# Score products of a streaming encoder's attention on 32 or 64 rows, two maps as a pair

## What is computed

```python
# B, per query block: keys selected by the indexer's top k
s = jnp.einsum('bqhd,bqkhd->bqhk', q, k_sel).astype(jnp.float32) * (B_HEAD_DIM ** -0.5)
p = jax.nn.softmax(jnp.where(valid[:, :, None, :], s, -jnp.inf), axis=-1)
...
# C, per query block: two maps i = 0, 1 of 32 channels per head
s = jnp.einsum('bqhid,bkhid->bhiqk', q, k).astype(jnp.float32) * (C_HALF ** -0.5)
p = jax.nn.softmax(jnp.where(mask, s, -jnp.inf), axis=-1)
attn = (p[:, :, 0] - lam * p[:, :, 1]).astype(v.dtype)
o = jnp.einsum('bhqk,bkhe->bqhe', attn, v)
```

## Time and profile before

| | us |
|---|---|
| median of 3 runs | 2077.38 |
| range of the runs | 2076.96 to 2079.85 |
| span of the profiled execution | 2076.9 |
| busy: TensorE | 1871.0 |
| busy: VectorE | 1235.4 |
| busy: ScalarE | 538.1 |
| busy: GpSimd | 311.5 |

### The profile page before, as it was taken

One profiled execution on the slowest core, in us unless ns is written; L12 is line 12 of the kernel. 1 busy time (PEld: TensorE's weight loads), 2 busy tenths in 40 slices (PEclk: granted clock), 3 DMA queues, 4 the chain that ended last, 5 costly groups with the idle time before them and its releaser, 6 DMA issues. The chain is left out here.

```text
span 2076.9 us, 21666 instructions
## 1 busy us (share of the span) xinstructions
PE 1871.0 (90%) x7650; PEld 1139.7 (55%) x7650; DVE 1235.4 (59%) x2634; ACT 538.1 (26%) x940; POOL 311.5 (15%) x389
## 2 busy tenths in 40 slices
PE   2999998999988999999839999989999888899997
PEld 2445454558864545666424455535588545566663
DVE  3158997099975445555240699961999644455551
ACT  2054005100023223333020631141010232333330
POOL 1000005040011123110120000052200111221111
PEclk8966999999989999999959679999999999999999
DMA  7000100101040211000150001101100402010000
GB/s 237 24 23 1 41 21 21 41 21 41 21 177 1 82 31 41 21 21 1 41 166 23 21 1 41 41 0 41 41 21 21 178 1 97 16 41 21 21 21 31
DMA packets 21476, 90.79 MB, mean 44 GB/s; under 512 B 4656, under 2 KB 9264, under 8 KB 16368
## 3 DMA queue, kind: packets, MB, share of 16 engines
q1 hardware_dynamic: 21376, 89.44, 12.5%
HBM read 71.30 MB, written 22.59 MB: 45 GB/s over the span
## 5 line engine op out<-in xcount | busy, mean ns | idle before, releaser
L1114 PE MATMUL ps<-r_xn,r_w 128*128 128x512 f32 (+1 forms) x1824 | 604.8, 495 | 9.0 <-ACT r_vg L774 6.5
L1114 PEld LDWEIGHTS ps<-r_xn,r_w 128*128 128x128 f32 x1824 | 304.7, 194 | 309.1 <-issue 306.9
L953 DVE TENSOR_SCALAR_CACHE_REDUCE r_ix<-r_sc,smi 128x384 bf16<-128x384 f32 x434 | 405.3, 999 | 2.2
L1057 DVE TENSOR_REDUCE sm<-ps 128x1 f32<-128x384 f32 (+8 forms) x216 | 174.7, 813 | 175.1 <-PE ps L1251 88.3
L818 ACT ACTIVATE r_sc<-ps,sm 128x384 f32<-128x384 f32 (+8 forms) x216 | 170.3, 789 | 365.9 <-DVE sm L1057 365.1
L1206 PE MATMUL ps<-r_w,r_xn 128*128 128x256 f32 (+1 forms) x1152 | 251.4, 380 | 0.0
L1206 PEld LDWEIGHTS ps<-r_w,r_xn 128*128 128x128 f32 (+1 forms) x1152 | 210.8, 184 | 39.8 <-issue 5.0
L1281 PE MATMUL ps<-r_vg,r_w 128*128 128x64 f32 (+1 forms) x1184 | 154.8, 275 | 20.7 <-DVE r_w L448 11.1
L1245 PE MATMUL ps<-r_qk,r_ix 128*128 128x128 f32 (+4 forms) x608 | 159.2, 395 | 15.7 <-POOL r_ix L602 11.9
L1281 PEld LDWEIGHTS ps<-r_vg,r_w 128*128 128x128 f32 (+1 forms) x1184 | 143.6, 192 | 38.5 <-DVE r_w L411 21.4
L1264 PE MATMUL ps<-ident,r_sc 128*128 128x128 f32 (+1 forms) x720 | 116.9, 271 | 35.3 <-ACT r_w L411 17.1
(11 more groups left out here) (173 smaller groups left out, 1833.7 us busy)
## 6 DMA issues: line engine op xcount, KB each, us to landing
r_w<-w_in SPq DMA_DIRECT2D x28, 1024.0 KB, 4.8
r_vg<-y SPq DMA_DIRECT2D x16, 512.0 KB, 3.9
xres<-y SPq DMA_DIRECT2D x16, 512.0 KB, 4.2
r_xn<-w_out SPq DMA_DIRECT2D x2, 4096.0 KB, 12.2
y<-r_res SPq DMA_DIRECT2D x16, 512.0 KB, 2.9
o_k<-r_qk SPq DMA_DIRECT2D x4, 1088.0 KB, 16.3
y<-x SPq DMA_DIRECT2D x8, 512.0 KB, 8.2
r_xn<-ckT SPq DMA_DIRECT2D x2, 2048.0 KB, 7.5
```

The lines of the kernel that those rows point to most:

```text
L953: ins = vec.tensor_scalar(unsel[t][0:rows(t), :], sc[t][0:rows(t), :], b, None, ALU.is_ge, ALU.add, accum_out=cnt[0:rows(t), c:c + 1])
L1057: vec.tensor_reduce(negm[0:r, c:c + 1], on_slot(s, w, r), X, ALU.max, negate=True)\
L1114: ins = nc.tensor.matmul(on_slot(key)[:, c0:c0 + cn], w[:, k, P * s:P * (s + 1)], xnT[:, k, c0:c0 + cn], start=(k == 0), stop=(k == KT - 1))
```

## The change

The zero padding goes: `qpc`, `qpb`, the copies on GpSimd and their semaphores. The score products read the queries and keys of a map at the 32 or 64 rows where they lie (`qk[rg, ...]`, `kTc[rg, ...]`), so the two maps of a C head, or the maps of B heads h and h+1, use different rows of the array. They are issued as a pair: TensorE waits until both slots are free, then issues piece 0 of the first map, piece 0 of the second, piece 1 of the first, and so on, and all mask products behind. `schedule()` puts both maps of a pair at one place, B heads 0 and 1 in the step of C head 3, B heads 2 and 3 in the step of B head 1, none in the steps of B heads 0 and 2. The buffers `ex` and `rden` are numbered anew for that. What VectorE, ScalarE and TensorE compute otherwise is unchanged.

```diff
     def qk(i):
-        return [("qk", i, m) for m in range(2 if units[i][1] == "C" else 1)]
+        if units[i][1] == "C":
+            return [("qk", i, 0), ("qk", i, 1)]
+        return [("qk", i, 0), ("qk", i + 1, 0)] if units[i][2] % 2 == 0 else []
...
-        steps += nxt[:1]
+        steps += nxt
         pv = [("pv", i - 1)] if i else []
         if len(groups) == 1:
             steps += pv
         if finish:
             steps.append(("rows", finish.pop(0)))
-        steps += nxt[1:] + fill + groups[:1]
+        steps += fill + groups[:1]
...
+def ex_of(i, m):
+    h = ATT[i][2]
+    return 2 * (i % 2) + m if ATT[i][1] == "C" else 2 * (h // 2 % 2) + h % 2
+
+PAIR = {MAPS[n]: MAPS[n:n + 2] for n in range(0, len(MAPS), 2)}
...
-                    pool.wait_ge(sel_ready, len(SCORED))
-                    nc.gpsimd.memset(qpc, 0.0)
-                    nc.gpsimd.memset(qpb, 0.0).then_inc(qp_zero, 1)
-                    pool.wait_ge(qp_zero, 1)
-                    for key in (("fm", "cq", 0), ("fm", "cq", 1), ("fm", "bq", 0), ("fm", "bq", 1)):
-                        wait_drained(pool, key)
...
-                    pad_c(0)
-                    pad_b(0)
...
                             if i >= 2:
-                                last = TJOB[("tr", i - 2, groups_of(i - 2) - 1)]
+                                before = i - 3 if kind == "B" and h % 2 else i - 2
+                                last = TJOB[("tr", before, groups_of(before) - 1)]
                                 act.wait_ge(t_filled, last + 1)
...
-                            wait_free(s)
-                            if kind == "C":
-                                q, kk = qpc[:, h % 2, m, h // 2, 0:r], QK0["ck"] + h // 2
-                            else:
-                                q, kk = qpb[:, h % 2, h // 2, 0:r], QK0["bk"] + h // 2
-                            if h == 0 and m == 0:
-                                pe.wait_ge(qc_ready if kind == "C" else qb_ready, i // 8 + 1)
+                            for key in PAIR[s]:
+                                wait_free(key)
...
+                            kd = CHALF if kind == "C" else DB
+                            last = {}
                             for c0, cn in parts:
...
+                                for key in PAIR[s]:
+                                    h, m = ATT[key[1]][2], key[2]
+                                    g = 2 * (h % 2) + m if kind == "C" else h % 2
+                                    rg = slice(kd * g, kd * (g + 1))
...
+                                    last[key] = nc.tensor.matmul(on_slot(key)[0:r, c0:c0 + cn],
+                                                                 qk[rg, qq + h // 2, P * t:P * t + r], keys,
+                                                                 start=True, stop=not (diag or masked is not None))
+                            for c0, cn in parts:
+                                for key in PAIR[s]:
+                                    out = on_slot(key)[0:r, c0:c0 + cn]
+                                    if masked is not None:
+                                        last[key] = nc.tensor.matmul(out, diagm[:, 0:r], masked[:, c0:c0 + cn],
+                                                                     start=False, stop=True)
+                                    elif t < SAMPLE and c0 + cn == w:
+                                        last[key] = nc.tensor.matmul(out, diagm[:, :], chunk[:, :], start=False, stop=True)
+                            for key in PAIR[s]:
+                                fills(last[key], key)
```

More of the change, by code:

```diff
@@ L268, in build @@
         den = sm[:, 156:160]
-        rden = sm[:, 160:164]
+        rden = sm[:, 224:232]
         mixc = sm[:, 164:166]
@@ L424, in combine @@
             d = [den[0:r, (f + m) % 4:(f + m) % 4 + 1] for m in range(2)]
-            rr = [rden[0:r, 2 * (i % 2) + m:2 * (i % 2) + m + 1] for m in range(2)]
+            rr = [rden[0:r, 2 * (i % 4) + m:2 * (i % 4) + m + 1] for m in range(2)]
             if kind == "B":
@@ L447, in divide @@
             yy = yt[n % 2][0:r, col:col + DC]
[L448 removed]
+            vec.tensor_scalar(yy, obank[0:r, :], rden[0:r, 2 * (i % 4):2 * (i % 4) + 1], None,
                               ALU.mult).then_inc(o_drained, 1)
@@ L810, in _ @@
                             i, m = s[1], s[2]
-                            t = ATT[i][0]
+                            t, kind, h = ATT[i]
                             r, w = rows(t), width(t)
@@ L1214, in _ @@
                     for s in STEPS:
-                        if s[0] == "qk":
-                            i, m = s[1], s[2]
-                            t, kind, h = ATT[i]
+                        if s[0] == "qk" and s in PAIR:
+                            t, kind, _ = ATT[s[1]]
                             r, w = rows(t), width(t)
@@ L1221, in _ @@
                                 seen_sample = True
-                            wait_free(s)
-                            if kind == "C":
-                                q, kk = qpc[:, h % 2, m, h // 2, 0:r], QK0["ck"] + h // 2
-                            else:
-                                q, kk = qpb[:, h % 2, h // 2, 0:r], QK0["bk"] + h // 2
-                            if h == 0 and m == 0:
-                                pe.wait_ge(qc_ready if kind == "C" else qb_ready, i // 8 + 1)
-                            cc = (2 if kind == "C" else 0) + h // 2
+                            for key in PAIR[s]:
+                                wait_free(key)
                             masked = unsel.get(t) if kind == "B" else None
@@ L1243, in _ @@
-                                out = on_slot(s)[0:r, c0:c0 + cn]
-                                diag = t < SAMPLE and c0 + cn == w and masked is None
-                                ins = nc.tensor.matmul(out, q, keys,
-                                                       start=True, stop=not (diag or masked is not None))
-                                if masked is not None:
-                                    ins = nc.tensor.matmul(out, diagm[:, 0:r], masked[:, c0:c0 + cn],
-                                                           start=False, stop=True)
-                                elif diag:
-                                    ins = nc.tensor.matmul(out, diagm[:, :], chunk[:, :], start=False, stop=True)
```

55 lines of the change are left out of this document (12 added, 43 removed).

## The result

The kernel before takes 2077.17 us (median of 4 runs, 2074.67 to 2079.85), the changed one 2163.09 us (4 runs, 2156.72 to 2166.20): 1.041 times the time, interval 1.039 to 1.043. The forecast of 2063 and its range up to 2092 missed it. The profiled execution of the changed kernel spans 2164.2 us.

What follows compares the result with a forecast made beforehand. TensorE was taken as the bound in steps with a projection, the map-reduction-exponential chain only a little shorter elsewhere. 2076.9 less 31.6 gained (15.8 a layer) plus 17.4 for clock drops gave 2063 us, range 2042 to 2092.

Steps and rivals of the forecast that it cites:

- (1): Start of attention: without GpSimd's padding the first reduction starts earlier, 5.2 us a layer won.
- (2): Score products: two maps on different row groups run together, a 1024-column C pair streaming 1.71 us instead of twice that.
- program order: Rival, chance 0.08: a pair's instructions start as issued, a a b b; 11 us a layer more, 2085 us.
- no overlap: Rival, chance 0.08: two-instruction products do not run side by side; 2138 us without any clock drop.
- (3): Score pairs: going from 128-row to 64-row operands and back costs 0.3 us a pair, 54 pairs a layer.
- (4): C steps with a projection, widths 640 to 1024: TensorE's work shrinks, 14.2 us a layer won.
- (5): C steps without projection: 0.35 us a step won at 384 and 512 columns, 2.6 us a layer.
- (6): B steps: new order makes TensorE wait for VectorE's evacuation, 8.9 us a layer lost; C 3 with B 0 wins 2.2.
- (7): TensorE's clock in attention: five more drops a layer at 1.74 us each, 8.7 us a layer, 17.4 in all lost.
- Stays low into the next pair: Rival, chance 0.17: clock falls at all nine places a layer, half lasting on at 2.6 us each; 2092 us.

Runs made afterwards that it cites:

- h2: Kernel before with only C heads 1 to 3 of tiles 4 to 7 as row-tiled pairs and the first tile's C head 0 unpadded: 2049.31 us.
- h4: h2 with the first tile's C head 0 padded again: 2057.24 us.
- h0: Kernel before with only the first tile's first C head on its own 32 rows instead of the padded copy, no pairs: 2077.35 us (1.000).
- h0b: h0 once more, the same kernel: 2075.25 us (0.999).
- e1: Kernel before with its order kept, each map issued by itself, but products on own 32 or 64 rows and no GpSimd padding: 2315.24 us (1.113).
- e2: Changed kernel's order with pairs, but on zero-padded 128-row operands again, a pair's maps in turn: 2221.82 us (1.068).
- e5_late: Changed kernel with the second B map of a pair reduced and exponentiated at its own head's step: 2083.58 us (1.003).
- e8: e5_late with all maps on zero-padded 128-row operands: 2132.98 us (1.027).
- h5_late_wide: h2 with B heads of tiles 4 to 7 as row-tiled pairs too, the second map handled at its own head's step: 2040.27 us (0.982).
- e7_fill32: Changed kernel with useless 32-row products added beside the B heads' waits in tiles 4 to 7: 2176.60 us.
- e6_fill128: Changed kernel with useless 128-row products added beside the B heads' waits in tiles 4 to 7: 2136.76 us.

## Why the prediction was wrong, step by step

(1) *Start*: right where it was read, though it shows in the time only beside pairs (8 us in h2 against h4, nothing clear in h0 and h0b). TensorE computes the first pair at 591.63, and the reduction starts 5.9 us earlier than the 599.75 of the earlier trace rows, where 5.2 was said (timeline of the changed kernel):

```profile
591.63 0.92 PE L1213 MATMUL ps<-r_qk 32*128 32x256 f32 x8 [0.56 <-ACT r_vg L771]
...
593.87 1.02 DVE L1025 TENSOR_REDUCE sm<-ps 128x1 f32<-128x384 f32 x2
```

(2) *Overlap*: right. In the pair at 989.55 the single instructions of the trace start in twos, 989.549 and 989.556, 990.082 and 990.089. The trace doesn't name the map. In the kernel before a map's own two instructions start 0.43 us apart (950.85 and 951.28), so I read these twos as one of each map, though the kernel's text issues each product's two instructions together. The rule of strict program order (the Trainium skill, "TensorE: Matmul & The Clock Gate", Part 3) does not describe the order of these starts. The rivals of program order and of no overlap are out.

(3) *Shape change*: right, 0.3 us. From the last transpose's start to the first product's (989.346 to 989.549) it is 0.20 us, and 0.20 from the last product's to the mask's, where two transposes in a row start 0.11 apart. Between the first 512-column instructions of a map on own rows stand 0.53 us (989.549 to 990.082), between later ones, and between padded ones, 0.43. That is 0.09 + 0.10 + 0.09. e1's single maps show the same three figures, e2's padded pairs none of them.

(4) *C steps with projection*: right to 0.1 us where the clock is high (7.16 and 8.24). In the time of a whole kernel, h4, which has this part alone, is 21 us faster where 28.4 had been summed.

(5) *C steps without projection*: wrong. A gain of 0.35 us a step was given to the narrow tiles. In the changed kernel tile 2's C heads run at a granted clock of 0.50 from the first head on, and from the first head's division to B head 0's it is 16.4 us instead of 10.9. The kernel before starts this tile at 1.2 GHz as well, but is back after 13.7 us (593.9 to 607.6); the changed one stays there for 68 (596.5 to 664.8).

(6) *B steps*: the mechanism was right, waits included: 1.91 us at 768, 2.01 at 896 and 2.10 at 1024 columns where 2.5 was said for 1024, and C head 3 with B head 0 take 10.85 us at 768 (885.59 to 896.44) against the 11.0 of the text. Two B steps take 10.68 (896.44 to 907.12) instead of 8.9, and 1.2 of the 1.8 between are the value products at the low clock. The sample tile, counted at 0.7, has 5.2 us more of idle time (13.4 against 8.2 from its first division to the next tile's), with these two waits in it:

```profile
671.29 0.50 PE L1237 MATMUL ps<-ident,r_sc 64*128 64x64 f32 x4 [3.85 <-ACT r_w L418]
...
686.87 0.46 PE L1237 MATMUL ps<-ident,r_sc 64*128 64x64 f32 x4 [2.64 <-DVE r_w L418]
```

In e5_late the idle time is 8.2 us again, so they come from the second B map ahead. I had worked the queues out for the wide tiles alone.

(7) *The clock*: the step that failed, by the price of a fall and not by their number. Five more drops a layer were said. By the counts of above it is 10 against 3 in layer 1 and 11 against 5 in layer 2, seven and six more. The price, 1.74 us, was taken from one place of the kernel before. Even there it was read too low, since it has only the first map behind the wait. The next map paid too, and so did the transposes (0.69 for 0.46), 2.5 us in all:

```profile
640.62 2.43 PE L1245 MATMUL ps<-r_xn,r_ix 128*64 128x512 f32 x4
...
649.07 1.88 PE L1245 MATMUL ps<-r_xn,r_ix 128*64 128x512 f32 x4
```

More than that, this place had padded maps right behind the wait, and during the second of them the clock came back (6.8 us at 1.2 GHz). The change takes exactly these maps away. With pairs on 32 rows in their place one fall cost 7.0 us (tile 5, above), and it took a projection to end it; the narrow tiles, which have none, run at low clock for most of 590 to 720 us. "Stays low into the next pair" was the slow rival, with half its drops lasting on at 2.6 us each: the right direction, and too small by more than two. The earlier trace rows prices a fall with its end right behind it, and that end was in what the change removes. The sum had 31.6 us to gain; the gains of (1) and (4) were 38.8 of it, and h2, which makes these two parts only, has 28. The clock, with the waits of (5) and (6), took more than 100 us in the changed kernel: stretches at 1.2 GHz sum to 199 and 196 us in the two layers, against 14 and 17 before.

What stays open: by how much each of the two, rows and waits, would do harm without the other cannot be added up (e2 against e8: the late second map is worth 89 us on padded rows, e5 against the changed kernel 79.5 on own rows, own rows 59 and 49). Why the clock falls in e1 with no wait ahead, for the 32 rows as such or because single maps on them stand longer in the stream than pairs do, was not separated either.

## What to carry to other kernels

A product's cost is its time and what it does for TensorE's clock. Before taking rows or padding out of products, mark on the timeline which full products end each low stretch now, and price a fall by the time to the next full ones that stay, over all work in between. Count falls and their length apart: here the count was nearly right. Put row-tiled pairs only where long full products follow and no new wait stands ahead of them, and check on the helper engines that nothing (a reduction, an exponential) is queued before a copy that TensorE waits for: h5_late_wide, which does both in the wide tiles, is at 2040 us (0.982 of the time before, 0.979 to 0.984) the fastest here.

## What the runs showed of the hardware

- What TensorE does in a wait bears on its granted clock, and not only that it is busy. Behind useless products on 32 rows twelve value products took 2.66 us, behind the same products on 128 rows 1.45, and the kernels differ by 40 us (e7_fill32, e6_fill128).
- The clock fell with no wait ahead in e1_rows_alone, where single maps on 32 rows went from 1.77 to 2.81 us.
- With the same order a stretch at 1.2 GHz lasted some 7 us behind padded products and 15 to 20 us on own rows (e2_padded_pairs and e8_padded_late against the changed kernel and e5_late).
- Products on different row groups overlap though the kernel's text issues their instructions a a b b, and start 6 to 7 ns apart (989.549 and 989.556). Going from 128 to 32 rows and back costs 0.09 us at each end and 0.10 at the first product, some 0.3 us a pair.
